# A new weaving plan for the mixer steps of a streaming encoder kernel, and two attention items in the score banks

## What is computed

```
u = rmsnorm(x) @ w_in                       # split into the inputs of A, B and C
A: p = softmax(q k^T) for two maps; out = (p0 - lam * p1) @ v        # 6 heads, block-causal
B: score = sum_h w_h * relu(qi_h ki^T); keep the best 256 keys (or 136) of a frame;
   out = softmax over the kept keys @ v                              # 5 heads
C: gated linear recurrence over blocks of frames                     # 5 heads
x += concat(rmsnorm(A), B, rmsnorm(C) * silu(gate)) @ w_out
x += (silu(conv(h @ up_a)) * (h @ up_g)) @ w_down,  h = rmsnorm(x)
```

## Time and profile before

| | us |
|---|---|
| median of 3 executions | 4685.71 (4683.24 to 4696.35) |
| profiled execution, its time | 4685.55 |
| its span (first to last instruction) | 4683.8 |
| TensorE busy | 4061.7 (87% of the span) |
| VectorE busy | 2274.1 (49%) |
| ScalarE busy | 1010.0 (22%) |
[...]

### The profile page before, as it was taken

One profiled execution on the slowest core, in us unless ns is written; L12 is line 12 of the kernel. 1 busy time (PEld: TensorE's weight loads), 2 busy tenths in 40 slices (PEclk: granted clock), 3 DMA queues, 4 the chain that ended last, 5 costly groups with the idle time before them and its releaser, 6 DMA issues.

```text
span 4683.8 us, 47834 instructions
## 1 busy us (share of the span) xinstructions
PE 4061.7 (87%) x19244; PEld 2695.9 (58%) x19244; DVE 2274.1 (49%) x4647; ACT 1010.0 (22%) x2288; POOL 222.0 (5%) x172
## 2 busy tenths in 40 slices
PE   7988777887889998898899888854799998989998
PEld 5754336766667776773344444334577777744443
DVE  1731444499843555428634545399324445432222
ACT  1113222211023332211132222010133322211001
POOL 3111100000000002200000000400000000000000
PEclk9997777988999998899998989977899998999999
DMA  3321121211121212221121211321111111121222
GB/s 135 106 92 53 52 67 41 64 54 39 64 64 47 72 36 79 90 89 66 62 86 37 70 49 59 100 64 63 45 42 59 69 58 49 59 82 64 75 76 73
DMA packets 142165, 310.33 MB, mean 66 GB/s; under 512 B 29160, under 2 KB 69608, under 8 KB 130680
## 3 DMA queue, kind: packets, MB, share of 16 engines
q1 hardware_dynamic: 81432, 262.25, 17.1%
q10 hardware_dynamic: 60512, 45.02, 3.4%
HBM read 271.08 MB, written 36.14 MB: 66 GB/s over the span
## 4 chain that ended last, share of the span: by engine, by line
PE 71%; DVE 22%; ACT 2%; issue 2%; DMA 1%; ACTq 1%; SPq 0%; DVEq 0%
PE PS L572 49%; DVE scr L1191 7%; DVE top L1190 6%; PE PS L579 5%; PE PS L668 4%; PE PS L641 3%; PE PS L657 3%; PE PS L629 2%; PE PS L548 2%; PE PS L759 1%; PE PS L690 1%; PE PS L758 1%; DVE mx L1211 1%; DVE inv L1128 1%; DMA kv<-out_projN 1%
## 5 line engine op out<-in xcount | busy, mean ns | idle before, releaser
L572 PE MATMUL PS<-xn,wring 128*128 128x272 f32 (+1 forms) x6048 | 1925.7, 480 | 116.1 <-DVE xn L1131 51.2
L572 PEld LDWEIGHTS PS<-xn,wring 128*128 128x128 f32 x6048 | 1193.5, 199 | 807.4 <-issue 598.2
L572 PE MATMUL PS<-dense,wring 128*128 128x272 f32 (+1 forms) x2112 | 666.5, 474 | 35.6 <-DVE xT L1137 32.4
L572 PEld LDWEIGHTS PS<-dense,wring 128*128 128x128 f32 x2112 | 408.7, 197 | 266.1 <-issue 205.1
L579 PE MATMUL PS<-wring,xn 128*128 128x224 f32 (+1 forms) x1728 | 361.9, 372 | 77.2 <-ACT dense L830 77.2
L1137 DVE TENSOR_TENSOR xT<-PS,xT 128x272 f32<-128x272 f32 (+1 forms) x240 | 123.9, 523 | 558.2 <-PE PS L572 557.6
L579 PEld LDWEIGHTS PS<-wring,xn 128*128 128x128 f32 (+1 forms) x1728 | 327.4, 193 | 105.0 <-ACT dense L830 77.9
L1190 DVE MAX8 top<-scr 128x8 f32<-128x384 f32 (+6 forms) x418 | 367.7, 880 | 13.3
L1191 DVE MATCH_REPLACE8 scr<-top,scr 128x384 f32<-128x384 f32 (+6 forms) x418 | 359.8, 861 | 0.0
L668 PEld LDWEIGHTS PS<-kv,scr 128*128 128x128 f32 (+2 forms) x1804 | 226.6, 192 | 98.8 <-ACT scr L953 62.5
L572 PE MATMUL PS<-catT,wring 128*128 128x272 f32 (+1 forms) x768 | 235.0, 467 | 48.0 <-DVE xT L1137 42.6
(11 more groups left out here) (160 smaller groups left out, 3081.7 us busy)
## 6 DMA issues: line engine op xcount, KB each, us to landing
wring<-in_wu SPq DMA_DIRECT2D x88, 1024.0 KB, 4.8
wring<-in_wf SPq DMA_DIRECT2D x76, 512.0 KB, 3.4
wring<-in_wd SPq DMA_DIRECT2D x64, 384.0 KB, 3.1
wring<-in_wn SPq DMA_DIRECT2D x24, 896.0 KB, 4.9
wring<-in_wd SPq DMA_DIRECT2D x64, 320.0 KB, 2.9
wring<-in_wo SPq DMA_DIRECT2D x32, 512.0 KB, 3.3
kv<-out_projT ACTq DMA_DIRECT2D x48, 256.0 KB, 4.2
out_projN<-dense SPq DMA_DIRECT2D x96, 112.0 KB, 1.7
```

The source lines that it names most:

```text
L572: mm = nc.tensor.matmul(PS[:, dbank(t.g0 + j), 0:cw], wtile(t.q, i), rhs, start=(kk == a), stop=(kk == b - 1))
```

## The change

The plan is made by a new function, `weave`, and the segments are joined: P00 and P01 take the steps of m = 0, F00 and P10 those of m = 1, F01 those of m = 2, and P11, F10 and Y0 those of m = 3. A step gets turns in proportion to the time that TensorE is expected to wait in it (0.3 us, plus the longer of its ScalarE and VectorE work, or a stated wait, less its own TensorE work), and none before its inputs exist (`first`). Loading for selection becomes a step of its own, ahead of `dots`, with a wait of 9 us to be covered, and so does B's `entry`. Attention steps are given little: for B items of half 1 the need is 0.2 us, for its A items under 1 us.

For A items with at most 512 keys, two items lie in the banks by turns (`abank`), and scores of item s wait only for item s - 2. For even m the order in an attention step becomes scores, transposes, values.

```
+def turn_time(t):
...
+    pe = 13.3 * wide * (5.5 / 8 if t.kind == "dn" else 1)
...
+def step_times(kind, m):
...
+            if what == "load":
+                out.append((0, 0.5, 0, 9))
+            elif what == "pick":
+                out.append((0, 0, min(BURST, ROUNDS[h][y] - BURST * z) * 2 * (1.04 * k + 0.15), 0))
...
+            if it.g == "b":
+                out.append((5 * k + 0.3, 0.6 + 2.2 * k, 0.5 + 1.05 * k, 0))
+            else:
+                out.append((5 * k + 0.3, 0.9 + 3.2 * k, 1.3 + 4.6 * k, 0))
...
+def weave(dense, mixers):
+    steps = []
+    for kind, m in mixers:
+        l, h = PROJS[m]
+        first = F_TURN[l, h, 5] + 4 if kind == "X" else STAGE["P%d%d" % (l, h)][1] + 3
+        for pe, act, dve, wait in step_times(kind, m):
+            steps.append((first, 0.3 + max(wait, act + dve if kind in "CM" else max(act, dve)) - pe))
+    turns = [(i, max(0.5, turn_time(TURNS[i])[0])) for i in dense]
+    have, need = sum(t for i, t in turns), sum(max(0.2, t) for first, t in steps) or 1
+    plan, j, x, y = "", 0, 0.0, 0.0
+    for i, time in turns:
+        while j < len(steps) and i >= steps[j][0] and y / need <= (x + time / 2) / have:
+            y += max(0.2, steps[j][1])
+            plan, j = plan + "s", j + 1
+        plan, x = plan + "d", x + time
+    return plan + "s" * (len(steps) - j)
...
-    segment(_span("P01", 6), _steps("B00", "C00", "M00")),
...
-    segment(_span("F00", 4), _steps("X01", "B01")),
-    segment(_span("P10"), _steps("C01", "M01")),
...
-    segment(_span("P11", LEAD), _steps("X11")),
...
-    segment(_span("F10", 4) + _span("Y0"), _steps("B11", "C11", "M11")),
...
+    weave(_first[:LEAD], []) + weave(_first[LEAD:], STEPS[0:4]),
+    weave(turns_of("F00", "P10"), STEPS[4:8]),
+    weave(turns_of("F01"), STEPS[8:12]),
+    weave(_last[:LEAD], []) + weave(_last[LEAD:], STEPS[12:16]),
...
+        def abank(s, u, x):
+            return 2 * x if u.nk > 512 else 2 * (s % 2) + x
...
-                if items[s - 1].g == "a":
-                    pe.wait_ge(s_ex, M0[m][s])
+                before = s if u.nk > 512 or items[s - 1].unit.nk > 512 else s - 1
+                if items[before - 1].g == "a":
+                    pe.wait_ge(s_ex, M0[m][before])
...
-                        mm = nc.tensor.matmul(PS[:u.w, 2 * x + a // 512, 0:b - a], q[r, u.col:u.col + u.w], k[r, u.key + a:u.key + b],
+                        mm = nc.tensor.matmul(PS[:u.w, abank(s, u, x) + a // 512, 0:b - a], q[r, u.col:u.col + u.w], k[r, u.key + a:u.key + b],
...
+                if s < len(items) and m % 2 == 0:
+                    scores(s)
+                if s >= 3 and m % 2 == 1:
                     values(s - 3)
                 if 2 <= s < len(items) + 2:
                     turned(s - 2, 0)
-                if s < len(items):
+                if s < len(items) and m % 2 == 1:
                     scores(s)
+                if s >= 3 and m % 2 == 0:
+                    values(s - 3)
...
-                if what == "dots":
+                if what == "load":
```

More of the change, by code:

```diff
@@ L215, in _pick_steps @@
 def _pick_steps(h):
-    out = [("dots", 0, 0)]
+    out = [("load", 0, 0), ("dots", 0, 0)]
     for y, r in enumerate(ROUNDS[h]):
@@ L228 @@
 CT_COUNT = [sum(2 * len(UNITS[i % 2]) for i in range(m + 1)) for m in range(4)]
-def step_costs(kind, m):
+def turn_time(t):
+    wide = W[t.h] / 1000
+    if t.kind == "t":
+        return 3.0, 0.4, 0
+    if t.kind == "nsq":
+        return 6, 8 * 1.2 * wide, 0
+    if t.kind == "nsc":
+        return 6, 0.9, 18 * wide
+    if t.kind == "y":
+        return 0, 0, 0
+    pe = 13.3 * wide * (5.5 / 8 if t.kind == "dn" else 1)
+    return {"f": (pe, 1.7 * wide, 0), "wo": (pe, 0, 1.9 * wide), "dn": (pe, 0, 1.9 * wide), "a": (pe, 2 * wide, 0),
+            "g": (pe, 3.2 * wide, 9.5 * wide)}[t.kind]
@@ L248, in segment @@
[L248 to L262, removed]
@@ L265, in _steps @@
-def _steps(*names):
-    return [c for n in names for c in step_costs(n[0], PROJS.index((int(n[1]), int(n[2]))))]
+        out = []
+        for what, y, z in PICK_STEPS[h]:
+            k = PICKS[h][y].nk / 1000
+            if what == "load":
[3 more added lines that the diff above has]
+            else:
+                out.append((2 * k, 2.6 * k, 2.6 * k if what != "dots" else 0, 0))
@@ new lines, in step_times @@
+        return out
+    if kind == "B":
+        out = [(0, 1, 0, 9)]
+        for it in ITEMS[m]:
+            k = it.unit.nk / 1000
+            if it.g == "b":
+                out.append((5 * k + 0.3, 0.6 + 2.2 * k, 0.5 + 1.05 * k, 0))
+            else:
+                out.append((5 * k + 0.3, 0.9 + 3.2 * k, 1.3 + 4.6 * k, 0))
+        return out + [(1, 1, 0, 0)] * 3
+    w = W[h] / 1000
+    if kind == "C":
+        one = [(0, 2.4 * w + 1.3, 16 * w, 0), (0, 2.4 * w + 1.3, 5 * w, 0), (0, 3.5 * w, 4 * w, 0), (0.8, 4.4 * w, 4 * w, 0), (1.6, 2.4 * w, 4 * w, 0),
+               (2, 2.4 * w, 5.5 * w, 0), (2, 2.4 * w, 4 * w, 0), (1.5, 0, 4.5, 0), (3, 1.8, 0, 0), (0, 1, 0, 0)]
+        return one * 3
@@ new lines, in step_times @@
+    return [(0, 2, 1.5, 0), (0, 3, 1, 0), (0, 1.5, 1, 0), (0, 0, 1.5, 0)] + [(1.2, 1, 1.8, 0)] * len(UNITS[h])
+def weave(dense, mixers):
[14 more added lines that the diff above has]
+    return plan + "s" * (len(steps) - j)
@@ L269, with turns_of @@
+def turns_of(*names):
+    return [i for n in names for i in range(*STAGE[n])]
 LEAD = 12
+_first, _last = turns_of("P00", "P01"), turns_of("P11", "F10", "Y0")
+STEPS = [(kind, m) for m in range(4) for kind in "XBCM"]
 PLAN = "".join((
-    segment(_span("P00", 0, LEAD), []),
-    segment(_span("P00", LEAD), _steps("X00")),
-    segment(_span("P01", 0, 6), []),
-    segment(_span("P01", 6), _steps("B00", "C00", "M00")),
-    segment(_span("F00", 0, 4), []),
-    segment(_span("F00", 4), _steps("X01", "B01")),
@@ L285 @@
+    weave(turns_of("F01"), STEPS[8:12]),
+    weave(_last[:LEAD], []) + weave(_last[LEAD:], STEPS[12:16]),
+    weave(turns_of("F11", "Y1"), []),
 ))
-STEPS = [(kind, m) for m in range(4) for kind in "XBCM"]
 class Lane:
@@ L918, in idx_scalar @@
                             act.eng.dma_start(iw[:u.w, u.slot, :], projT[l, R_IW:R_IW + HI, c:c + u.w].rearrange("h t -> t h")).then_inc(x_in, 16)
+                elif what == "dots":
                     relu(0, 0)
```

22 lines of the change are left out of this document (4 added, 18 removed).

## The result

The new kernel takes 4711.6 us (median of six runs, 4705.7 to 4713.2), the one before 4687.8 (4680.4 to 4696.4): 1.0054 times as long, 95% interval 1.0043 to 1.0065. It is slower by 24 us. The forecast was 4648, faster; the time lies within the range, the sign was wrong. The profiled execution has a span of 4708.5 us against 4683.8.

What follows compares the result with a forecast made beforehand. TensorE, busy 87% of the span, was taken as the bound through its work, idle time and half-clock stretches. Gains of 240 us less losses of 202 made 38 less than 4685.6: 4648 us, range 4585 to 4750.

Steps and rivals of the forecast that it cites:

- Selection: Spreading selection's steps among turns removes TensorE waits: gains of 101 us (m = 3), 24 (m = 1) and 19 (m = 2).
- the loads: Selection's inputs and B's `entry`: earlier loads remove waits of 22.0 and 14.6 us and restarts, a gain of 40 us.
- rival 2: Selection still holds TensorE, since ScalarE's relu waits for VectorE's sums and blocks banks: no change, 4694 us; chance 0.10.
- Attention and recurrence of half 0: m = 0 gains 28 us in attention and 20 in recurrence; m = 2 gains 8 in recurrence, loses 45 in attention.
- A items of half 1: Attention m = 1 and m = 3: items directly behind another wait for it, 8.4 us on average; loss 157 us.
- B items of half 1: Attention m = 1 and m = 3: rows without turns were taken to stay at clock 1.00, with no loss priced.
- Rival 1: Attention m = 1 and m = 3: B items in rows lose the clock, 101 us more, 4749 us; chance 0.27.

Runs made afterwards that it cites:

- e2: The new kernel with the old banks and old order of TensorE's work in attention of half 0, plan and load steps kept: 4750.7 us.
- e7: The new kernel with one turn each in m = 1 and m = 3 moved from ahead of item s7 to ahead of s12: 4647.8 us.
- e13: The new kernel with the transposes of every B item of half 1 issued three times, same result: 4697.1 us.
- e8: The new kernel with the score matmuls of every B item of half 1 issued twice, same result: 4694.3 us.
- e10: The new kernel with turns put back between items of half 1, and selection's picks in steps of 2 rounds instead of 4: 4484.7 us.
- run 53: Not a label of a run: the words belong to "had run 53 us at 1.00", a time that B items spent at full clock.
- e5: The new kernel with only the need of A items of half 1 raised (5 us), so turns stand between them: 4574.9 us.

## Why the prediction was wrong, point by point

**Selection.** Forecast gains for m = 3, m = 1, m = 2 and the loads 101 + 24 + 19 + 40 = 184; measured in selection and the stretches ahead of m = 0: 118 + 39 + 27 + 15 = 199. The estimates of what would stay were 69 for m = 1 (69.3) and 45 for m = 3 (36.9). Right, but for m = 1 partly by luck: what stays was met, while today's loss is 108 by the table and was taken as 93, so 39 were gained and not 24. (The four long waits of the earlier trace rows add up to 137.6 us and not 138.6; the gain was taken from the idle time, so nothing hangs on it. And VectorE was 69 and 74% busy in the spread selections, not over 80 as rival 2 had it.) PE's waits in the window of selection m = 3, where four long ones stood in the earlier trace rows:

```profile
PE PS L600 <- DVE xT L1173: 21.6, 6, 5.8
PE PS L600 <- DVE xn L1167: 3.7, 1, 3.7
PE PS L626 <- ACT scr L933: 1.4, 1, 1.4
```

What was late next was named rightly: adds of `dn` turns behind picks, three times 4.7 to 5.8 us. No wait for `iw` is left, and of those at `entry` only one, 8.6 us, as written.

**Attention and recurrence of half 0.** Forecast 28 + 20 + 8 gained, 45 lost; measured 26, 32, 24 and 51 (the two recurrences with their merges). Recurrence m = 1, for which nothing was written, gained 19. In attention m = 0 the A items gave 20 of the 23 written, though from 137.5 to 117.2 us and not from 127 to 104, since the banks brought 1.4 us an item and not 2.5 (e2); the B items cost 15 of 13, and the restarts made it up. The two recurrences were sized 12 and 16 too low, that of m = 2 beyond its bound of 20.

**A items of half 1: the term was too small.** 157 were written (136 and 29, less 8), the A items and the restarts took 180 + 8. The period was right, and 33 items stand behind another where 31 were written; but those of 1024 keys mostly took 9.4 to 10.3 us, and two of m = 1 took 14 and 15, where a norm of the next projection got in between: at the end of s35 TensorE waits 4.4 us for its squares on ScalarE, in s40 7.2 us for maxima that stand behind its scaling on VectorE.

**B items of half 1: the failed step.** The prediction gave these items no cost. It took 3374 to 3388 us of the earlier trace rows, three items with short pauses at 1.00, as the picture of a whole row. But that was 14 us out of a plan where a turn follows behind the first or second item, and only there behind the third. A pause even longer than that of the new kernel did no harm in it, where a turn stood right behind (clock 1.00 from 3440 to 3455 us):

```profile
3444.43 0.44 PE L657 MATMUL PS<-ident,scr 128*128 128x128 f32 x2 [1.73 <-ACT scr L953]
3444.70 7.50 PE L572 MATMUL PS<-xn,wring 128*128 128x272 f32 x32
```

In a row of thirteen without a turn, more waits follow it, and TensorE stays at half clock, busy 94%. Rival 1 named this, its place (the pause of `load_pair` in the middle of a row) and the reason. It took 13 items of each m at 3.9 us more each, 101 us; 8 B items of each m fell, at 3.9 more each, 62 us, and 64 with the small changes of the other B items. Of the 3.9, 3.4 are the clock, by the same items at 1.00 in e7. The other 14 us are the last three steps of attention, for which nothing was written.

**The sum.** Gains 300 instead of 240, losses 326 instead of 202. Of the 124 that the losses were short, 64 are the B items of rival 1, 31 the A items' size, 14 the last steps, 8 what comes after attention m = 3, 6 attention m = 2. All but rival 1 are 60, as much as the gains were short, and so e7, where the B rows keep the clock, takes the 4648 us that were forecast: the sign turned on that one step. That the two errors of 60 cancel is luck; the recurrences (12, 16 and 19 too low) and selection (15) had nothing to do with the A items. The chance of 0.30 for slower was too small for what the earlier trace rows held: one window that spoke for rival 1 and one against it.

That transposes as such made the clock fall was not shown, and the runs speak against it here: three times the transposes held the clock as doubled matmuls did (e13 and e8, both at 1.00). That the pause of s11 got shorter too in e13 leaves some doubt.

## What to carry to other kernels

A plan that gives turns by a step's own waiting must price what the step costs without a turn, not the time of its longest engine: for the A items of half 1 that was a chain over three engines (8.8 us an item behind another, 4.0 with a turn between), for the B items a clock that one pause of 1.36 us took away (3.9 us more an item). Put a piece of dense work right behind a pause that can't be removed (two moved turns gave 64 us in e7). Ask of every step how long it holds the engine that others need between their turns; where it is longer than a turn, halve it (50 us in e10).

## What the runs showed of the hardware

TensorE at half clock did not come back by being busy with these items: 65 us at 94% busy stayed at 0.50 until a turn came, while such items at 87% busy, with one turn among them, had run 53 us at 1.00. A turn brought it back: 67 turns began at half clock in the new kernel's trace, and each ended at full. The pause that tipped it was 1.36 us with 0.47 behind it; waits of 0.4 to 0.7 us, one in each item, did not. The margin is thin, and the waits alone don't settle it: 0.78 and 0.37 us at the head of a row tipped it once in e5 and not in the new kernel, 0.74 and 0.47 tipped it in m = 1 of e7 while 0.84 and 0.47 did not in m = 3, and the executions of e5 ranged over 50 us (4528 to 4580). What else it takes stays open. And added work made the kernel faster: 1.1 to 1.7 us more in each of most of the 40 B items of half 1 made it 15 to 17 us shorter.
